# Attention of the prompt in layer 0: on TensorE the scores of the unit two ahead are issued in front of the present unit's transposes

## The reference, cut to what matters

```python
def mla_attend(q_lat, q_rope, ckv, krope, q_pos, k_pos):
    s = (jnp.einsum('bqhc,bkc->bhqk', q_lat, ckv)
         + jnp.einsum('bqhr,bkr->bhqk', q_rope, krope)).astype(F32) * MLA_SCALE
    s = jnp.where(k_pos[None, None, None, :] <= q_pos[None, None, :, None], s, -jnp.inf)
    p = jax.nn.softmax(s, axis=-1).astype(ckv.dtype)
    return jnp.einsum('bhqk,bkc->bqhc', p, ckv)
...
    o_lat = mla_attend_blocked(q_lat, q_rope, k_ckv, k_rope, pos, k_pos)
    yb = jnp.einsum('bthc,chv->bthv', o_lat, w_uv).reshape(b, t, MLA_WIDTH)
```

## Time and profile before

| what | us |
|---|---|
| median of 3 runs | 3364.31 |
| lowest and highest run | 3359.61, 3364.52 |
| the profiled execution | 3363.42 |
| its span, first to last instruction | 3361.8 |
| the stage of the 64 units within it (first scores to last values) | 501.5 to 802.0 |

### The profile page before, as it was taken

How to read it: one execution, slowest core, us unless ns; L and a number is a source line. 1 busy time by engine, 2 the same in 40 slices (tenths; PEclk the granted TensorE clock), 3 DMA queues, 4 the chain that set the end, 5 groups by cost and what they waited for, 6 DMA issues and landing times. The chain is left out here.

```text
span 3361.8 us, 42138 instructions
## 1 busy us (share of the span) xinstructions
PE 2825.5 (84%) x16534; PEld 2223.9 (66%) x16534; DVE 1568.0 (47%) x2711; ACT 822.6 (24%) x1492; POOL 589.3 (18%) x436
## 2 busy tenths in 40 slices
PE   5997856665998989988889978978589999699889
PEld 5996633334766779956689966755455554499566
DVE  3999624443554430045355643105576775300353
ACT  3223413332221322222233221101122221221221
POOL 2222210001331321102222200000121222221012
PEclk8998978898998989989999989987799999799999
DMA  2311540003552002213022221126533321121151
GB/s 84 95 45 53 181 148 0 0 1 129 175 173 80 1 26 74 83 75 126 5 83 96 84 99 62 70 65 225 142 88 101 95 74 15 32 69 39 60 203 46
DMA packets 237204, 277.40 MB, mean 83 GB/s; under 512 B 44870, under 2 KB 183815, under 8 KB 231316
## 3 DMA queue, kind: packets, MB, share of 16 engines
q1 hardware_dynamic: 217234, 186.84, 18.3%
q0 software_dynamic: 16384, 75.77, 6.3%
q10 hardware_dynamic: 3456, 12.98, 1.0%
HBM read 230.51 MB, written 45.47 MB: 82 GB/s over the span
## 5 line engine op out<-in xcount | busy, mean ns | idle before, releaser
L305 PE MATMUL pp<-HH,WS_part 128*128 128x352 f32 x1824 | 589.1, 323 | 0.0
L303 PE MATMUL pp<-HH,WH 128*128 128x352 f32 x1344 | 436.4, 325 | 30.2 <-POOL WS_part L444 30.2
L304 PE MATMUL pp<-HT_part,WH 128*128 128x352 f32 x1344 | 434.4, 323 | 0.0
L305 PEld LDWEIGHTS pp<-HH,WS_part 128*128 128x128 f32 x1824 | 345.3, 189 | 0.0
L303 PEld LDWEIGHTS pp<-HH,WH 128*128 128x128 f32 x1344 | 254.3, 189 | 32.0 <-POOL WS_part L444 32.0
L2658 PE MATMUL OP<-oWO,YT 128*128 128x512 f32 (+1 forms) x576 | 252.5, 597 | 3.3 <-DVE XE L2785 3.3
L304 PEld LDWEIGHTS pp<-HT_part,WH 128*128 128x128 f32 x1344 | 254.5, 189 | 0.0
L444 POOL TENSOR_TENSOR WS_part<-WS,WH 128x1024 fp32r<-128x1024 f32 x56 | 143.1, 2555 | 504.1 <-ACT WH L395 504.1
L816 DVE SCALAR_TENSOR_TENSOR CV<-GX,cw,CV x360 | 215.9, 676 | 0.0
L2658 PEld LDWEIGHTS OP<-oWO,YT 128*128 128x128 f32 (+1 forms) x576 | 103.8, 182 | 144.0 <-issue 140.1
L1976 DVE TENSOR_REDUCE xmx<-xS 128x4 f32<-128x1024 f32 x16 | 19.5, 1219 | 377.4 <-PE xS L1937 377.4
(11 more groups left out here) (490 smaller groups left out, 5498.0 us busy)
## 6 DMA issues: line engine op xcount, KB each, us to landing
WS<-x_w_qg SPq DMA_DIRECT2D x32, 512.0 KB, 4.0
HT<-cache_mem_k SPq DMA_DIRECT2D x16, 1024.0 KB, 8.1
HT<-cache_mem_v POOLq DMA_DIRECT2D x16, 1024.0 KB, 9.0
CBt<-cum_scratch SPq DMA_DIRECT2D x8, 2048.0 KB, 10.0
xbc_scratch<-oACC ACTq DMA_DIRECT2D x24, 528.0 KB, 2.7
WS<-o_w_in SPq DMA_DIRECT2D x24, 512.0 KB, 3.9
XT<-xbc_scratch SPq DMA_DIRECT2D x8, 1536.0 KB, 7.6
WS<-e_w_in SPq DMA_DIRECT2D x20, 512.0 KB, 4.0
```

The lines of the kernel that those rows point to most:

```text
L303: nc.tensor.matmul(out, wh, xh, start=start, stop=False)
L304: nc.tensor.matmul(out, wh, xl, start=False, stop=False)
L305: return nc.tensor.matmul(out, wl, xh, start=False, stop=stop)
```

## The change

In the PE list of `mla_prompt` the scores of the unit two ahead are issued before the transposes of the present one, for both units of a step. At i = 6 the projections of the keys stay behind the transposes of the even unit, and the scores that stood behind them now stand ahead of both. Nothing else is altered: the waits inside `scores`, `turn`, `ahead` and `values`, and the lists of DVE, ACT, POOL and SP are the same.

```diff
                 scores(1)
                 for s in range(NU // 2):
                     j, i, _ = unit(2 * s)
+                    if 2 * s + 2 < NU:
+                        scores(2 * s + 2)
                     turn(2 * s)
-                    if 2 * s + 2 < NU:
-                        if i == 6 and j + 1 < PAIRS:
-                            ahead(j + 1, i)
-                        scores(2 * s + 2)
-                    turn(2 * s + 1)
+                    if i == 6 and j + 1 < PAIRS:
+                        ahead(j + 1, i)
                     if 2 * s + 3 < NU:
                         scores(2 * s + 3)
+                    turn(2 * s + 1)
                     if i != 6 and j + 1 < PAIRS:
                         ahead(j + 1, i)
                     values(s)
```

## The result

| | before | after |
|---|---|---|
| median, us | 3361.96 (4 runs) | 3266.29 (4 runs) |
| lowest and highest, us | 3359.03, 3364.52 | 3262.93, 3267.67 |
| profiled execution, its span, us | 3363.42, 3361.8 | 3262.93, 3261.3 |
| stage of the 64 units to the next block's first load, us | 301.0 | 210.6 |
| its granted clock | 0.91 | 0.98 |

The ratio is 0.9714, with a 95% interval of 0.9697 to 0.9731: the change takes 95.7 us off. The forecast was 3280, with a range of 3267 to 3303. The direction and the mechanism held, and the time came out 13.7 us under the forecast and 0.7 us under the low end of the range; the prediction had given 0.04 to a time under 3268. Two executions, one of the kernel before at 4333.31 us and a granted clock of 0.63 and one of a later kernel at 5216.47 us and 0.78, are slower than all the others by far, and the medians and ratios in this text leave them out.

What follows compares the result with a forecast made beforehand. It took a chain alternating between PE and DVE to bound the stage. A gain of 73 us at full clock and 11 of clock loss given back made 84, so 3280 us, with a range of 3267 to 3303.

Steps and rivals of the forecast that it cites:

- The bound: Stage of the 64 units: a chain going back and forth between PE and DVE, with waits of 100.2 and 97.1 us.
- The sum at full clock, 73 us: Stage gain at full clock: 43 and 15.6 us in three pairs with projections, 14.4 in the last pair.
- The layout: All 64 units laid out by full-clock durations from the trace: stage of 279 us before and 206 after.
- The new wait, some 10 us: Values on PE wait for ACT's copies of PT, which the odd unit's scores covered before; counted in the 73 us.
- The clock, 11 us given back: Stage's clock loss of 21.5 us: half expected back, the middle between all of it and none.
- What lies behind the stage: All after the stage, from the next block's first load: expected to shift earlier by what the stage saves.
- (a): Rival: the stage's clock loss of 21.5 us stays or grows a little; gain 65 to 73 us, chance 0.20.
- (b): Rival: DVE's wait for the projection holds the chain, odd half gains nothing there; 17 us less gain, chance 0.06.
- (c): Rival: nothing changes, as scores already start before the transposes or the exponential is later; 3364 us, chance 0.03.
- (d): Rival: slower, as PE stays at 1.2 GHz and becomes the bound; stage 339 us, time 3403, chance 0.02.
- The signs: Expected in the profile after: stage 216 us, step 5 7.7, line 1433 wait 30, copies' wait 10, scores' wait nearly gone.

Runs made afterwards that it cites:

- filler run: The kernel before with two useless matmuls in front of each unit's transposes, where PE waits for DVE: 3345.51 us, ratio 0.9954.
- the first of the two later edits: The changed kernel with the values of a step issued behind the first scores of the next step: 3260.84 us, ratio 0.9702.
- the even half: The kernel before with only the even unit's scores brought forward, the odd unit's order kept: 3293.88 us, ratio 0.9793.
- the odd half: The kernel before with only the odd unit's scores brought forward, the even unit's order kept: 3315.58 us, ratio 0.9869.

## Why the prediction was right or wrong, point by point

**The bound.** Right. PE and DVE waited for each other in turn, and both waits fell to about a fifth when the scores came forward.

**The sum at full clock, 73 us.** Right, and in its parts. From the even unit's transposes to the next step's, steps 0 to 7 of a pair with projections take at full clock 6.08, 7.12, 8.16, 9.22, 10.26, 11.31, 14.00 and 7.04 us in the old order (step 6 from the filler run, where the clock stays full, the others from the kernel before) and 5.05, 5.40, 5.90, 6.42, 6.98, 7.87, 9.58 and 6.25 in the changed one. The gains are 1.0, 1.7, 2.3, 2.8, 3.3, 3.4, 4.4 and 0.8, and the prediction had 1.1, 1.6, 2.2, 2.7, 3.2, 3.6, 4.4 and 0.8. Added up over the stage such steps, with what stands ahead of the first and behind the last as it ran, give 281.6 us for before and 209.3 for after, so 72 for the difference. The layout had 279.6 and 206.6 (279 and 206, and 0.6 to the next load); it is 2 to 3 us short on both sides, which cancels.

**The new wait, some 10 us.** Right in place and about right in size: 8.3 us in all, 0.8 of it there before, and the first of the two later edits shows that it was paid.

**The clock, 11 us given back.** This is the term that failed. The prediction held both bounds, all of 21.5 us or none, and took the middle, since "the two kinds of rows speak about equally". In fact nearly all came back. Against the full-clock steps added up above, before lost 19.4 us (301.0 less 281.6), or 22.9 in its second profile, and after lost 1.3 (210.6 less 209.3). That makes 18 to 22 us instead of 11, so 7 to 11 us too little gain in the forecast. The rows that were weighed against it were the first 20 us, "slow before PE had waited long for DVE", which "will be slow again". Of them 17 had been at the lower clock (0.36 and 0.49 of ten us, twice), and after the change some seven were (0.34, twice). The filler run shows why the middle was the wrong choice: the falls of the clock go when PE has more to do where it waited, and the change, which takes most of these waits away, took nearly the whole loss along. Each half of the change by itself, which leaves 44 or 60 us of PE's waits, still lost clock (some 6 us for the even half, by such steps).

**What lies behind the stage.** The prediction carried it over unchanged, and the median of before with it. In the two profiled executions, 3279.4 forecast and 3262.93 measured, 6 of the 16.5 us between them lie in the stage and 10 behind it: the profiled execution of before had the longest form of the state block (214.3 us against 207.1). One more run moved the median of before from 3364.31 to 3361.96. In the medians, 95.7 us, the stage's 90 to 94 us leave only 2 to 5 for the rest. The range's low end, a gain of 97 from 3364.3, allowed for the whole clock loss and 3 us of spread. The gain from that base was 98.0, so that even the whole clock loss given back (279 to 206, and 21.5: a gain of 94.5) would have left it 3.5 us short. A spread of 10 us behind the stage, or of 3.5 in the stage of before, could not be seen in one profile; three runs from 3359.6 to 3364.5 did hint at it.

**The rivals.** (a), that the clock loss stays, fell: 0.98. The rule of the Trainium skill that stood beside it (TensorE: Matmul & The Clock Gate, section "A second HAM failure mode: psum-queue depth-cycling") agrees with the stage before, where short idles and a clock that moves between its levels go together. For the stage after it gave a kept loss, and there PE still has 36 short waits for the normalising and 11 for the copies, none over 0.9 us, and three of 1.3 us for the copies of the keys, and the clock stays full from 510 us on; the measurement decides. (b) fell, by the odd half's gain. (c) and (d) fell by the time.

**The signs.** Step 5 (7.87 for 7.7) and the wait for the copies (8.3 for some 10) came as written. The stage was 210.6 for some 216, and PE's wait for line 1433 fell to 17.3 us, not to 30. DVE's wait for the scores fell to 20.4, which isn't nearly gone.

## What to carry to other kernels

Where two engines alternate in a chain, look for the instruction in the queue that needs only an early result and stands behind one that needs a late result, and put it in front. Here the gain could be laid out from the starts in a few steps' rows, to 0.2 us a step. If the stage also loses granted clock, test first by fillers whether PE's idle time causes it. Where it does, as here, a change that takes most of that time away can give nearly the whole loss back, and half of it is a poor forecast. And before a range is set, take the base from more than one profile: here the part that the change doesn't touch varies by 10 us.

## What the runs showed of the hardware

Two matmuls more for each unit, 128 in all, made the kernel 16.6 us faster, because the granted clock of the stage went from 0.91 to 0.99 while the critical chain kept its order. PE's waits for the normalising summed to 43.0 us there and to 44.3 in the even half alone, and only in the second did the clock still fall behind the first step (0.96). The state block took one of three lengths, 207, 211 or 214 us, in ten executions of eight kernels; its mean granted clock was 0.74 in the shortest form and 0.72 in the longest.
